# A hybrid SSM and convolution decoder layer on one core: C tables turned on VectorE, splits and additions of the 15-product passes in another order, down-projection groups fed one quarter ahead

## What is computed

```python
h = x + 0.5 * swiglu(rmsnorm(x, ffn1_norm), w_gate1, w_up1, w_down1)     # 1024 -> 2816 -> 1024
p = rmsnorm(h, mix_norm) @ w_in
s_out = s5_mixer(p[..., :512], ...)      # diagonal complex SSM, 32 groups x 64 states
c_out = short_conv_mixer(...)
h = h + concat([s_out, c_out]) @ w_out
h = h + 0.5 * swiglu(rmsnorm(h, ffn2_norm), w_gate2, w_up2, w_down2)
y = rmsnorm(h, final_norm)
```

## Time and profile before

| | before |
|---|---|
| median of 3 runs | 1913.75 us (1909.55 to 1920.72) |
| the profiled execution's own time | 1914.03 us |
| its span, first to last instruction | 1911.2 us |
| mean granted TensorE clock | 0.964 |
| PE busy, matmuls | 1778.4 us (93%), 11761 |
| DVE busy | 1293.3 us (68%) |
| ACT busy | 680.0 us (36%) |
| POOL busy | 772.6 us (40%) |
| DMA moved | 151.43 MB, mean 79 GB/s |

### The profile page before, as it was taken

One profiled execution on the slowest core, in us unless ns is written; L12 is line 12 of the kernel. 1 busy time (PEld: TensorE's weight loads), 2 busy tenths in 40 slices (PEclk: granted clock), 3 DMA queues, 4 the chain that ended last, 5 costly groups with the idle time before them and its releaser, 6 DMA issues.

```text
span 1911.2 us, 31212 instructions
## 1 busy us (share of the span) xinstructions
PE 1778.4 (93%) x11761; PEld 1755.1 (92%) x11761; DVE 1293.3 (68%) x2145; ACT 680.0 (36%) x1269; POOL 772.6 (40%) x767
## 2 busy tenths in 40 slices
PE   8998799999767777799999999999999999999998
PEld 8998799999657777799999999999999999999998
DVE  7264677776755555466257755997778877887775
ACT  7211444444322222235221153543333333333333
POOL 2697455555383233321079812223323333233320
PEclk9999899999878888899999999999999999999999
DMA  5432223222522022124811170111111111112112
GB/s 151 167 117 87 83 72 91 77 64 92 188 78 78 25 84 80 56 67 175 153 35 46 55 226 12 51 45 52 53 52 51 50 51 51 55 45 61 45 41 104
DMA packets 182358, 151.43 MB, mean 79 GB/s; under 512 B 11538, under 2 KB 175698, under 8 KB 181188
## 3 DMA queue, kind: packets, MB, share of 16 engines
q1 hardware_dynamic: 176724, 141.80, 24.3%
q0 software_dynamic: 864, 5.28, 0.8%
q10 hardware_dynamic: 4624, 2.36, 0.5%
HBM read 117.86 MB, written 31.57 MB: 78 GB/s over the span
## 4 chain that ended last, share of the span: by engine, by line
PE 74%; POOL 11%; DVE 5%; DMA 4%; issue 3%; ACT 2%; SPq 0%; DVEq 0%; POOLq 0%; ACTq 0%
PE bank_pair L1502 20%; PE bank_pair L1504 20%; PE bank_pair L1503 20%; PE bank_down L1502 4%; PE bank_down L1504 4%; PE bank_down L1503 4%; POOL PROD L3757 3%; DMA GW_raw<-in_ffn_w_down 3%; POOL UF_raw L3896 1%; POOL BS L3757 1%; POOL CA L3757 1%; ACT GS_hi L2329 1%; DVE GH_lo L3098 1%; POOL GS_raw L3903 1%; POOL TMP L3757 1%
## 5 line engine op out<-in xcount | busy, mean ns | idle before, releaser
L1502 PE MATMUL bank_pair<-XHM,U_hi 128*128 128x344 f32 x720 | 230.4, 320 | 0.2 <-DVE XLM L2870 0.2
L1504 PE MATMUL bank_pair<-XHM,U_lo 128*128 128x344 f32 x720 | 229.7, 319 | 0.0
L1503 PE MATMUL bank_pair<-XLM,U_hi 128*128 128x344 f32 x720 | 229.7, 319 | 0.0
L1502 PEld LDWEIGHTS bank_pair<-XHM,U_hi 128*128 128x128 f32 x720 | 135.2, 188 | 0.6 <-DVE XLM L2870 0.5
L1503 PEld LDWEIGHTS bank_pair<-XLM,U_hi 128*128 128x128 f32 x720 | 135.2, 188 | 0.0
L1504 PEld LDWEIGHTS bank_pair<-XHM,U_lo 128*128 128x128 f32 x720 | 135.2, 188 | 0.0
L1502 PE MATMUL bank_pair<-XF_hi,UF_hi 128*128 128x344 f32 x340 | 111.4, 328 | 21.7 <-DVE UF_lo L3033 13.7
L1502 PE MATMUL bank_pair<-GH_hi,GS_hi 128*128 128x344 f32 x160 | 59.5, 372 | 69.0 <-DVE HT L3120 69.0
L1502 PE MATMUL bank_pair<-XH,WH 128*128 128x344 f32 x384 | 123.6, 322 | 0.1
L3240 DVE SCALAR_TENSOR_TENSOR HT<-bank_pair,HT 128x344 f32<-128x344 f32 x210 | 103.5, 509 | 28.3 <-PE bank_pair L1504 28.0
L1503 PE MATMUL bank_pair<-XL,WH 128*128 128x344 f32 x384 | 122.5, 319 | 0.0
(11 more groups left out here) (487 smaller groups left out, 5855.3 us busy)
## 6 DMA issues: line engine op xcount, KB each, us to landing
GW_raw<-in_ffn_w_down SPq DMA_DIRECT2D x20, 512.0 KB, 3.5
GH_raw<-h_scratch SPq DMA_DIRECT2D x25, 344.0 KB, 6.0
RAW<-in_w_in SPq DMA_DIRECT2D x16, 512.0 KB, 4.3
UN<-in_ffn_w_gate SPq DMA_DIRECT2D x30, 256.0 KB, 3.6
UN<-in_ffn_w_up SPq DMA_DIRECT2D x30, 256.0 KB, 3.1
DQ_raw<-in_ffn_w_down SPq DMA_DIRECT2D x30, 256.0 KB, 2.8
h_scratch<-SA SPq DMA_DIRECT2D x40, 172.0 KB, 2.0
U_raw<-in_ffn_w_gate SPq DMA_DIRECT2D x22, 256.0 KB, 2.9
```

Of the source, the lines that this page charges most:

```text
L1502: pe.matmul(out, wh, xh, start=first, stop=False, skip_group_check=onto)
L1503: pe.matmul(out, wh, xl, start=False, stop=False, skip_group_check=onto)
L1504: return pe.matmul(out, wl, xh, start=False, stop=last, skip_group_check=onto)
```

## The change

Four things change; the arithmetic of the result stays the same, and so do PE's products, but for the order of two in each pass.

1. **C turned by DVE.** Eight `c_turn(n)`, 6 two-input operations of 128x256 each, stand in `ffn_first` behind the reciprocal; POOL's turning of C is gone. C goes to DRAM from SP in block 3, and the first raw weights are loaded in block 5, no longer behind the first stage. The powers of A are made by POOL right after B. The order of the x steps on DVE is shifted to later blocks, and the rests of the x forms to single steps of the first pass.
2. **Passes.** R12 before R11. In a step DVE does the additions first, then the split of the step three ahead, then the products of the step before; ACT copies first.
3. **Groups, one quarter ahead.** ACT and DVE prepare the sums of quarter k+1, not k+2; the copy GW_hi of k+2 comes last in ACT's quarter. SP's loads at the end of the last pass stand in another order.
4. **Two low parts on POOL.** GH_lo of B13 and B23 (GH_0_lo, GH_1_lo) are made by POOL behind the sums and GW_lo of a quarter.

```diff
-PASS_ORDER = ("R1", "R2", "R9", "R4", "R6", "R3", "R7", "R0", "R5", "R8", "R13", "R14", "R11", "R12")
+PASS_ORDER = ("R1", "R2", "R9", "R4", "R6", "R3", "R7", "R0", "R5", "R8", "R13", "R14", "R12", "R11")
+BY_POOL = (B13, B23)
+GROUP_LOW = tuple(u for u in GROUP_FORMS if u not in BY_POOL)
+C_TURNS = 4 + 6 * 8
@@ SP
+                if f == 3:
+                    sp.wait_ge(c_done, C_TURNS)
+                    sp.dma_start(CAD, CA[:, :, :, :].rearrange("p g r n -> p (g r) n")).then_inc(ca_out, 16)
+                if f == FO - 2:
+                    sp.wait_ge(ca_out, 16)
+                    sp.wait_ge(bs_out, 32)
+                    for at in range(5):
+                        load_raw(0, at)
...
+            store_h(LAST, 1, 2)
+            run_past("R12")
+            load_ht(2, 5, DC)
+            run_past("R11")
+            load_group_h(0, B13)
+            sp.wait_ge(un_ready, len(RUN))
+            load_group_h(0, B23)
+            store_h(LAST, 2, 1)
+            store_h(LAST, 2, 2)
+            run_past(TAIL)
+            load_group_w(1)
+            for u in (B11, None, B22, B21):
+                load_group_h(1, u)
+            store_h(LAST, 2, 0)
@@ ACT
             for i in range(tail):
+                run_copies(i)
                 if i + 4 < tail:
                     run_hi(i + 4)
-                run_copies(i)
...
+            quarter_high(1)
             for k in range(4 * GROUPS):
                 g, q = divmod(k, 4)
-                if k == 0:
-                    quarter_high(1)
-                    sums_high(1)
-                if k + 2 < 4 * GROUPS:
-                    quarter_high(k + 2)
-                    sums_high(k + 2)
+                if k + 1 < 4 * GROUPS:
+                    sums_high(k + 1)
                 if g + 1 < GROUPS and q > 0:
                     for u in GROUP_FORMS[3 * (q - 1):3 * q]:
                         group_high(g + 1, u)
+                if k + 2 < 4 * GROUPS:
+                    quarter_high(k + 2)
@@ DVE
+            def c_turn(n):
+                cr, ci = (AP8[:, 7, what, :].rearrange("p (g o) -> p g o", o=1).broadcast_to([P, GP, C16]) for what in range(2))
+                x, y = (CA[:, :, ri, (n - 1) * C16:n * C16] for ri in range(2))
+                before = 4 + 6 * (n - 1)
+                dve.wait_ge(c_done, before)
+                for out, part, turn in zip(CTMP, (x, y, y, x), (cr, ci, cr, ci)):
+                    dve.tensor_tensor(out[:, :, :], part, turn, ALU.mult).then_inc(c_done, 1)
+                dve.wait_ge(c_done, before + 2)
+                dve.tensor_tensor(CA[:, :, 0, n * C16:(n + 1) * C16], CTMP[0][:, :, :], CTMP[1][:, :, :], ALU.add
+                                  ).then_inc(c_done, 1)
+                dve.wait_ge(c_done, before + 4)
+                dve.tensor_tensor(CA[:, :, 1, n * C16:(n + 1) * C16], CTMP[2][:, :, :], CTMP[3][:, :, :], ALU.subtract
+                                  ).then_inc(c_done, 1)
...
             for i in range(tail):
+                run_adds(i)
                 if i + 3 < tail:
                     run_lo(i + 3)
-                run_adds(i)
-                run_muls(i)
+                if i in late:
+                    x_form_lo(late[i])
+                if i > 0:
+                    run_muls(i - 1)
...
-                if name == "M1" and k == 0:
-                    sums_low(1)
-                if name == "M3" and k + 2 < 4 * GROUPS:
-                    sums_low(k + 2)
+                if name == ("M3" if k else "P2") and k + 1 < 4 * GROUPS:
+                    sums_low(k + 1)
@@ POOL
-            pool.wait_ge(c_done, 4)
-            for j in range(1, 9):
-                rotate(ca(0, j), ca(1, j), ca(0, j - 1), ca(1, j - 1), ar, ai, -1)
-            pool.dma_start(CAD, CA[:, :, :, :].rearrange("p g r n -> p (g r) n")).then_inc(ca_out, 16)
+            pool.wait_ge(c_done, C_TURNS)
...
+            for k in range(4 * GROUPS):
+                g, q = divmod(k, 4)
                 mix_sums(k)
                 quarter_low(k)
+                if k == 0:
+                    for u in BY_POOL:
+                        group_low(0, u)
+                elif g > 0 and q < 2:
+                    group_low(g, BY_POOL[q])
```

More of the change, by code:

```diff
@@ L281, in form_base @@
 def form_base(p):
-    return len(GROUP_FORMS) * GROUPS + sum(len(forms_of(i)) for i in range(p))
+    return len(GROUP_LOW) * GROUPS + sum(len(forms_of(i)) for i in range(p))
 def mixed_count(p, form):
@@ L399, in _counts @@
         ended[i][1] = dve
-        if t % 2 == 1:
-            for m, j in FINALS.get(name, ()):
-                dve += 1
-                final[t, m, j] = dve
+        if i > 0:
+            before, last = RUN[i - 1]
+            if before % 2 == 1:
+                for m, j in FINALS.get(last, ()):
+                    dve += 1
+                    final[before, m, j] = dve
+    before, last = RUN[-1]
+    for m, j in FINALS.get(last, ()):
+        dve += 1
+        final[before, m, j] = dve
     return first, final, ended
@@ L527, in hybrid_trunk @@
                 "R11": X_RAW["B11"]}
+        CTMP = [place(50304 + n * 1024, f"CTMP{n}", [P, GP, C16]) for n in range(4)]
         XF = {"R1": place_split(2176, "XF1", FORM, HALF), "R4": place_split(13184, "XF4", FORM, HALF),
@@ L1348, in _ @@
             load_group_w(3)
-            for u in (B11, None, B21, B22, B13, B23):
+            for u in (B13, B23):
                 load_group_h(1, u)
@@ L2208, in x_form_hi @@
                 if name == "R0":
-                    act.wait_ge(ca_out, 16)
+                    act.wait_ge(bs_out, 32)
                 if name == "R9":
@@ L2258, in ffn_first @@
                         discretise()
+                    if f == 6:
+                        for i in range(3):
+                            run_hi(i)
                     silu(f, (1, 2))
-                    if f == 6:
-                        x_form_hi("R0")
                     if f + 1 < FO:
@@ L2992, in ffn_first @@
                 x_restore("B01", 0, 1)
+                dve.wait_ge(bs_out, 32)
+                x_negative("R13", raw["R13"], raw["R12"], b["B02"], "B01")
                 first_split(0, 5)
[L2994 removed]
                 mul(4, 0)
[L2996 removed]
+                x_plus("R8", raw["R8"], raw["R13"], b["B01"], "R13")
                 mul(4, 1)
[L2998 removed]
+                x_plus("R11", raw["R11"], raw["R13"], b["B11"], "R13")
                 mul(4, 2)
                 first_split(1, 5)
[L3001 removed]
                 x_step("R1", raw["R1"], b["B01"], b["B00"], "R8")
@@ L3012, in ffn_first @@
                 x_form_lo("R4")
-                mul(6, 0)
                 x_form_lo("R9")
                 x_form_lo("R0")
-                mul(6, 1)
-                run_lo(0)
-                run_lo(1)
-                mul(6, 2)
+                for i in range(2):
+                    run_lo(i)
+                for tb in range(TB):
+                    mul(6, tb)
+                run_lo(2)
             def run_lo(i):
@@ L3434, in _ @@
             ffn_first()
-            x_form_lo("R13")
-            run_lo(2)
-            x_form_lo("R10")
             tail = len(RUN)
+            late = {1: "R13", 2: "R10", 4: "R8", 6: "R11", 7: "R12"}
             for i in range(tail):
+                run_adds(i)
                 if i + 3 < tail:
                     run_lo(i + 3)
-                run_adds(i)
-                if i == 0:
-                    x_form_lo("R8")
-                if i == 1:
-                    x_form_lo("R11")
-                if i == 2:
-                    x_form_lo("R12")
-                run_muls(i)
+                if i in late:
+                    x_form_lo(late[i])
+                if i > 0:
+                    run_muls(i - 1)
                 if i == tail - 5:
                     group_mix(0, T1)
+                if i == tail - 4:
                     group_low(0, B11)
-                if i == tail - 4:
                     group_mix(0, T2)
+                if i == tail - 3:
                     group_mix(0, T4)
+                    group_low(0, T1)
+                if i == tail - 2:
+                    group_mix(0, T3)
                     sums_low(0)
-                if i == tail - 3:
-                    group_mix(0, T3)
-                    group_low(0, T1)
-                    group_low(0, B21)
-                if i == tail - 2:
-                    group_low(0, T2)
-                    group_low(0, B22)
-            group_low(0, B13)
-            group_low(0, B23)
-            group_low(0, T3)
-            group_low(0, T4)
+            run_muls(tail - 1)
+            for u in GROUP_LOW[2:]:
+                group_low(0, u)
             for n in range(GROUP_STEPS):
```

226 lines of the change are left out of this document (107 added, 119 removed).

## The result

| | before | after |
|---|---|---|
| median | 1913.01 us (4 runs) | 1822.13 us (4 runs, 1819.22 to 1823.61) |
| profiled execution: span | 1911.2 us | 1817.3 us |
| mean granted TensorE clock | 0.964 | 0.987 |
| PE busy | 1778.4 us | 1749.7 us |

The ratio after to before is 0.9518, with a 95% interval of 0.9486 to 0.9549: 91 us faster, where 113.7 were forecast. The time lies just above the forecast's own band (1789 to 1820 us) and inside the range for 8 in 10 (1770 to 1835).

What follows compares the result with a forecast made beforehand. PE was taken as the bound, with 166.7 us lost to idle time and low clock. Left 17 + 4 + 2 + 2 + 28 = 53, gain 113.7: span 1797.5, time 1800.3 us; forecast 1789 to 1820, 8 in 10 1770 to 1835.

Steps and rivals of the forecast that it cites:

- What bounds the kernel: Whole kernel: PE sets the end; its idle time and lower clock in the first FFN lose 166.7 us.
- C on DVE: First stage: turns at 0.88 us an operation beside POOL make three weight splits late, 17 us lost.
- The case without collision: First stage: C's turns fit beside POOL's turning of B, 17 us less, 1783 us; chance 0.2.
- The start of the passes: First seven steps of the first pass: the 26.5 us lost become 4.
- Passes: Next 140 steps: waits at bank_down for DVE's UB go, 13.4 us lost becomes 2 (0.5 to 5).
- Last steps: Last three steps of the passes: 12.7 us lost becomes 2 (0.5 to 5).
- Groups: The 20 quarters: waits for just-loaded sums and powers of A go, 114.1 us lost becomes 28 (14 to 60).
- The start: Start of the groups: late B23, M6 of quarter 0, GS_lo of quarter 1 and the clock cost 14 us.
- The three later steps from first to second quarter: Groups: each of four such steps costs 1.5 us idle and as much clock, 12 us in all.
- become the bound: Groups: DVE's two-input operations wait for POOL and DVE bounds the groups, 60 us lost, 1832 us; chance 0.15.
- Slower: First stage: turns on DVE undo the whole gain and 0.5% more from 3.5 us an operation; chance 0.03.
- The sum: Whole kernel: 53 of 166.7 us lost stay, a gain of 113.7, span 1797.5 us.

Runs made afterwards that it cites:

- b_behind_c: Changed kernel, but POOL turns B only when DVE has ended all turns of C: 1824.71 us.
- muls_now: Changed kernel, but DVE makes a step's products in that step again, behind its split, not one step later: 1807.14 us.
- load_first: Changed kernel, but SP asks for a pass's last raw block, (1, 1), ahead of the store of block (1, 2): 1808.87 us.
- joined_mix: Changed kernel with load_first, group_start, B's turns and write wait later, group mixes spread, and first group's mix T2 behind R12's additions: 1789.25 us.
- k_plus_2: Changed kernel with the third part alone undone: ACT and DVE prepare sums of quarter k+2 again: 1894.75 us.
- lows_dve: Changed kernel with the fourth part alone undone: the rests of B13 and B23 are DVE's again: 1817.31 us.
- group_start: Changed kernel, but HT's last part loads behind B23 and the rest of quarter 1's sums comes behind M7: 1816.37 us.

## Why the prediction was nearly right

**What bounds the kernel** held: PE's losses went from 166.7 to 72.0 us, and the span followed to within 1 us.

**C on DVE.** The mechanism was right and its size too large by half: 17 us forecast, 11.6 measured, one wait in place of three. The turns cost 0.80 us an operation (0.88 forecast; 0.36 alone, 0.33 forecast), and the first of them, while POOL still had operations of 16 elements, ended at 65.0, 3.5 us after its start, not 5.3. So turn 4 and the three products ended at 80.0 and not at 84.7, up(2) was in time, and only gate(3) was late. The run b_behind_c showed that POOL's operations make the price: the same CTMP rows fell to 418 ns. By the Trainium skill, page "SBUF — State Buffer", section "SBUF: two separate sides", the loser waits for the other's whole instruction, which I had put at 0.99 us a turn operation; the pitch measured is 0.80, and the rows agree in kind only. The case without collision (chance 0.2) is out. The start of the passes lost 3.7 us, 4 forecast.

**Passes.** Here a step failed: "13.4 becomes 2". The waits at `bank_down` that it names did go, all three. But the change also puts DVE's products one step later (`run_muls(i - 1)`), and I costed that move at nothing. Behind the product of block (1, 2) SP has its store, behind the store the last raw load of the next pass, and behind that R6's sum and the rest of R4: four waits of 2.2 to 3.5 us, and their clock. muls_now and load_first take 13.1 and 11.6 us off this stretch. By the starts of PE's matmuls these four places, with the slow matmuls behind them, lose 20 of the 24 us. Nor would the rest have come to 2 (0.5 to 5): in the two runs 11.0 and 12.5 us are still lost. Some 4 of them are in the first pass, where R8 waits 2.3 us for ACT (3.7 us lost there in the changed kernel). I did not see that one: ACT's copy at 217.88 stands behind an x form's first part, and that waited for DVE's rest of another form until 216.62. The other 6 to 8 are at R9 and R4 of the even passes; in load_first they are DVE's own order, in which R4's rest has products and an addition ahead of it.

**Last steps.** 5.5 us, forecast 2: mix T2, ahead of R12's additions, took 3.02 us beside POOL's GW_lo where I had it at a VectorE price alone. R10 waited 4.0 us, and not under 3. joined_mix shows that this wait was worth nothing: it only comes before another.

**Groups.** 27.2 us, forecast 28, by luck, from two errors that cancel. The third part, the distance of one quarter, is nearly all of the gain (k_plus_2: 72 us). The start was 18.4 us and not 14: 14.5 in quarter 0, where M6 began 14.9 us behind M1 (12 to 14 forecast), and 3.9 in quarter 1. B23 came when it was forecast: ACT begins its part at 520.19, 9.0 us behind R10's end (8 to 10). Too small was what stands behind it. DVE's two rests took 3.31 us beside POOL's two, where I had 0.9 each (without POOL's two, in lows_dve, the wait at M6 is 1.7 us shorter), and in quarter 1 PE waited 3.4 us for GS_lo, behind a mix of 2.88 us on DVE, where I had 1 to 2 us. That HT's 1.6 MB move beside B13 and B23 I had not priced apart; group_start, with HT behind them, has 3.9 us less of waiting at M6. The three later steps from first to second quarter cost 2.6 to 2.8 us each, 3 forecast, and the first of the four is in the start: 7.9 in place of 12. DVE did not become the bound, not even with 7 us more of work in lows_dve: that case is out.

**Slower** is out: it needed 3.5 us an operation, and measured were 0.80.

**The sum.** 19.0 us more were lost than forecast (72.0 against 53). 22.0 of them are the passes' and 3.5 the last steps'; C on DVE gives back 5.4, the groups 0.8 and the start of the passes 0.3.

## What to carry to other kernels

When work is moved by one step on one engine, follow its result into the queues that wait for it in order: a store that was just in time holds every load behind it. Where two engines slow each other down, separating them gains only if what waits for the later one is moved too. And a chain load, sum, copy, rest through four engines that each have time is cured by letting each queue touch only what was loaded a stage ago, not by making any of the engines faster.

## What the runs showed of the hardware

- Two-input operations of 256 elements on DVE and POOL, side by side, run in step, and DVE pays nearly all: 0.36 us apart alone, 0.80 beside POOL; POOL's are 0.74 us apart alone (three in 2.22 us, b_behind_c) and 0.80 in step. With DVE's operations of 1376 elements it is POOL that pays more: its PROD operations took 1.18 us on the mean from 60 to 125 us in b_behind_c (0.66 alone), DVE's 1.9 (1.6).
- The two loads of 344 KB for B13 and B23 took 7.2 and 7.7 us from issue to landing with a load of 1.6 MB issued 0.5 us ahead of the first, and 3.6 and 4.3 us with that load moved behind them (group_start).
- A short wait costs more than itself: load_first takes 7.4 us of idle time off PE at R4 and R9 (12.6 with the change, 4.1 and 1.1 in load_first) and 11.6 us off the stretch. Behind the wait of 3.53 us in pass 4, R4's twelve matmuls took 3.25 us in the changed kernel and not 1.89.
